# The down projection of a decoder layer as seven block products instead of eight, in three passes over the weights

## The chip, the cores and the metric

The kernel runs on one core of a Trainium2 chip. The metric is the device time in microseconds (us) of that core; a time given for a kernel is the median of several runs. Beside it stands one profiled execution of the same kernel, whose durations the prediction uses. The engines are named as the profile names them: PE is TensorE (PEld its weight loads), DVE is VectorE, ACT is ScalarE, POOL is GpSimd, and SP is the engine that issues the transfers from memory.

## What is computed

One decoder layer over 512 tokens of width 1024, in float32. Attention (two groups of heads) and its output projection come first; the change does not touch them. Then comes the MLP with a norm on both sides:

```python
D_MODEL = 1024
SEQ = 512
D_FF = 4 * D_MODEL
...
        h = h + rms_norm(mix @ w_out[l], attn_post_g[l])
        u = rms_norm(h, mlp_pre_g[l])
        a = jnp.square(jax.nn.relu(u @ w_up[l]))
        h = h + rms_norm(a @ w_down[l], mlp_post_g[l])
```

The up projection is 512x1024 by 1024x4096, the down projection 512x4096 by 4096x1024. In what follows `a` (the activations) is the left factor of the down projection and `w_down` the right one.

## The kernel before

**Three matmuls for one.** Every float32 operand is kept as a high part, rounded to the matmul's number format (fp32r), and a low part, the rest. `mm3` (L911) issues high x high, high x low and low x high into one PSUM bank. So each block of weights passes ACT, which writes the high part (`hi_part`, L388, recorded at L389), and then DVE, which subtracts it from the whole to give the low part (`lo_part`, L634, recorded at L635; `lo_scaled`, L637, recorded at L638, does it with a gain per row). The same is done to the activations.

**Up projection** (`up_step`, L590 on ACT and L878 on DVE; `up_block`, L1157 on PE). 32 blocks of 128 columns of `w_up`; each block is 24 matmuls (8 row blocks x 3) of 512 tokens. Two blocks share a chunk of weights of 1 MB. PE writes banks 0 to 3 in turn; ACT takes relu out of the bank (L599), DVE squares it into `act_sb` (L884). The factor 1/rms of the norm ahead of the MLP is not applied here. It is left out until the end of the down projection, where its square (`stat[:, 4, t, 3:4]`) multiplies the rows.

**Down projection** (`down_chunk`, L1191, and `down_rows`, L1185, on PE; `down_hi`, L608, on ACT; `down_lo`, L897, on DVE). 16 chunks of 1 MB, each 256 rows of `w_down` by all 1024 columns. A chunk gives 48 matmuls of 128x512: 4 tiles of 128 tokens x 2 row blocks x 2 column halves x 3. The results grow in all eight banks. For every chunk ACT writes `w_hi` (128x2048 elements) and `a_hi` (128x1024), DVE writes `w_lo` and `a_lo`. Both `w_hi`/`w_lo` and `a_hi`/`a_lo` have two buffers: ACT begins on chunk c when PE has ended chunk c-2 (`w_used`), that is, when PE begins chunk c-1. SP issues the transfer of chunk c+2 as soon as DVE has done the low part of chunk c. POOL has nothing to do in this stage but the small operations of the last norm.

**The end.** Per tile of 128 tokens: ACT sums the squares of both halves from the banks (`y_squares`, L576), POOL makes 1/rms (`rms`, L316), DVE multiplies and adds the residual (`scaled`, L849), SP stores.

Of the kernel before, what the change touches and what calls it, by code (L numbers as in the profile page):

```python
# [32 lines left out]
def build(nc, x, attn_pre_g, w_in, mla_q_norm_g, w_mla_q_up, mla_kv_norm_g, w_mla_kv_up, w_out,  # L33
# [21 lines left out]
    w_down_v = w_down[0].rearrange("(k p) n -> p k n", p=P)  # L55

# [16 lines left out]
    with ExitStack() as ctx:  # L73
# [17 lines left out]
        uT_hi = sb("uT_hi", [P, ND, S], F32R)  # L91
        uT_lo = sb("uT_lo", [P, ND, S], F32R)
# [130 lines left out]
        OUT_PIECES = {i: [i - 4] if i < HEADS else [2 * i - 12, 2 * i - 11] for i in range(4, 14)}  # L223

# [4 lines left out]
        def _(sp):  # L229
# [48 lines left out]
            with sp.Fori(1, NF // 4) as i:  # L278
# [19 lines left out]
        def _(pool):  # L298
# [17 lines left out]
            def rms(norm, t, n, n_sq, parts=1, by=None, squared=False):  # L316
# [58 lines left out]
        def _(act):  # L375
# [184 lines left out]
            def mlp_hi(j, r, gains=True):  # L560

                act.wait_ge(raw_in[j], (r - j) * 8 + 16)
                if gains:
                    for k in range(ND):
                        w = slice(256 * k, 256 * k + 256)
                        last = hi_part(w_hi[1 - j][:, w], raw[j][:, w], g_up[:, k:k + 1])
                else:
                    last = hi_part(w_hi[1 - j][:, :], raw[j][:, :])
# [689 lines left out]
```

## Time and profile before

| | us |
|---|---|
| median of 3 runs (610.76 to 610.95) | 610.81 |
| profiled execution, device time | 610.47 |
| profiled execution, span of the records | 608.5 |
| PE busy in it | 594.7 (98%) |
| DVE, ACT, POOL busy | 296.7, 268.0, 100.3 |
| down projection, first matmul to last | 428.1 to 602.7 |

The span is what the records of the profile cover; 2.3 us lie between it and the median and are taken to stay. An engine's busy time is an average over stages with different limits, so the stage that is changed has to be read by itself. A matmul of 512 columns is recorded with 389 ns, but successive ones start every 0.227 us, since they overlap in the array: the pace, not the recorded length, is what a matmul costs.

### The profile page before, as it was taken

What the parts mean: (1) busy time and instruction counts of PE and PEld (TensorE: products, weight loads), DVE (VectorE), ACT (ScalarE), POOL (GpSimd) and SP (SyncE); (2) the same over time, 40 slices, a digit from 0 to 9 for tenths busy, and PEclk for the clock granted to TensorE, in tenths of its full rate; (3) what the DMA queues carried; (4) which work ended last, traced back from release to release, by engine and by line L of the source; (5) the groups of instructions that cost most, each with busy time, mean ns of one, the idle gap of its engine ahead of it and who ended that gap; (6) DMA issues with size and microseconds to landing.
All of it is one profiled execution on the core that took longest, in us unless ns stands there. A gap on an engine that the chain in (4) does not pass through costs nothing.

```text
span 608.5 us, 8201 instructions
## 1 busy us (share of the span) xinstructions
PE 594.7 (98%) x2992; PEld 500.5 (82%) x2992; DVE 296.7 (49%) x587; ACT 268.0 (44%) x564; POOL 100.3 (16%) x167
## 2 busy tenths in 40 slices
PE   7999999999999999999999999999999999999996
PEld 7988898887777788998888888888888888888884
DVE  3458582788788408535433534334242332423345
ACT  5563262788898424264425344252321313213132
POOL 1153200346798101120000000000000000000011
PEclk9999999999999999999999999999999999999999
DMA  8441412000220084004232242323223131232303
GB/s 305 128 129 57 169 70 69 1 1 1 71 71 1 6 306 139 0 1 139 69 113 94 73 134 69 111 96 122 86 76 131 69 130 77 77 130 69 104 16 122
DMA packets 32826, 55.24 MB, mean 91 GB/s; under 512 B 3232, under 2 KB 21408, under 8 KB 32800
## 3 DMA queue, kind: packets, MB, share of 16 engines
q1 hardware_dynamic: 31760, 54.90, 26.9%
q8 instruction: 15, 0.25, 0.2%
q10 hardware_dynamic: 1040, 0.00, 0.1%
q14 instruction: 11, 0.09, 0.1%
HBM read 52.80 MB, written 2.10 MB: 90 GB/s over the span
## 4 chain that ended last, share of the span: by engine, by line
PE 92%; DVE 3%; ACT 2%; issue 1%; DMA 1%; SPq 0%; DVEq 0%; POOLq 0%; POOL 0%; ACTq 0%
PE bank L913 30%; PE bank L914 29%; PE bank L915 29%; PE bank L1083 2%; DVE pT_lo L635 1%; ACT probs L501 1%; DVE bank L767 1%; DMA x_sb<-in_x 1%; PE bank L919 1%; PE bank L1020 1%; PE bank L952 1%; DVE kT_lo L635 0%; PE bank L1036 0%; ACT uT_hi L389 0%; ACT pT_hi L389 0%
## 5 line engine op out<-in xcount | busy, mean ns | idle before, releaser
L913 PE MATMUL bank<-uT_hi,w_hi 128*128 128x512 f32 (+1 forms) x280 | 104.0, 371 | 0.0
L914 PE MATMUL bank<-uT_lo,w_hi 128*128 128x512 f32 (+1 forms) x280 | 103.8, 371 | 0.0
L915 PE MATMUL bank<-uT_hi,w_lo 128*128 128x512 f32 (+1 forms) x280 | 103.8, 371 | 0.0
L913 PE MATMUL bank<-w_hi,a_hi 128*128 128x512 f32 x256 | 99.7, 389 | 0.1
L914 PE MATMUL bank<-w_lo,a_hi 128*128 128x512 f32 x256 | 99.6, 389 | 0.0
L915 PE MATMUL bank<-w_hi,a_lo 128*128 128x512 f32 x256 | 99.6, 389 | 0.0
L635 DVE TENSOR_TENSOR w_lo<-w_raw,w_hi 128x2048 fp32r<-128x2048 f32 (+1 forms) x17 | 38.4, 2261 | 111.8 <-ACT w_hi L389 111.8
L389 ACT ACTIVATE w_hi<-w_raw 128x2048 fp32r<-128x2048 f32 (+2 forms) x25 | 37.0, 1490 | 118.7 <-PE bank L915 117.9
L638 DVE SCALAR_TENSOR_TENSOR w_lo<-w_raw,g_up,w_hi 128x256 fp32r<-128x256 f32 x128 | 52.1, 480 | 48.3 <-ACT w_hi L389 48.3
L599 ACT ACTIVATE relu<-bank 128x512 f32<-128x512 f32 x32 | 19.1, 598 | 98.2 <-PE bank L915 98.2
L322 POOL TENSOR_SCALAR stat<-stat 128x1 f32<-128x1 f32 x8 | 1.9, 239 | 363.9 <-ACT junk_post L414 363.9
L913 PE MATMUL bank<-w_hi,uT_hi 128*128 128x512 f32 (+1 forms) x160 | 61.9, 387 | 0.0
L915 PE MATMUL bank<-w_hi,uT_lo 128*128 128x512 f32 (+1 forms) x160 | 61.1, 382 | 0.0
L914 PE MATMUL bank<-w_lo,uT_hi 128*128 128x512 f32 (+1 forms) x160 | 61.0, 382 | 0.0
L913 PEld LDWEIGHTS bank<-uT_hi,w_hi 128*128 128x128 f32 x280 | 52.8, 188 | 9.1
L915 PEld LDWEIGHTS bank<-uT_hi,w_lo 128*128 128x128 f32 x280 | 52.8, 188 | 9.1
L914 PEld LDWEIGHTS bank<-uT_lo,w_hi 128*128 128x128 f32 x280 | 52.8, 188 | 8.9
L389 ACT ACTIVATE w_hi<-w_raw,g_up 128x256 fp32r<-128x256 f32 x128 | 52.7, 498 | 12.5 <-DMA w_raw<-in_w_up 12.2
L913 PEld LDWEIGHTS bank<-w_hi,a_hi 128*128 128x128 f32 x256 | 48.1, 188 | 10.4 <-issue 0.5
L915 PEld LDWEIGHTS bank<-w_hi,a_lo 128*128 128x128 f32 x256 | 48.1, 188 | 10.0
L914 PEld LDWEIGHTS bank<-w_lo,a_hi 128*128 128x128 f32 x256 | 48.1, 188 | 9.9
L884 DVE TENSOR_TENSOR act_sb<-relu 128x512 f32 (+1 forms) x32 | 22.1, 690 | 64.6 <-ACT relu L599 64.6
(127 smaller groups left out, 944.6 us busy)
## 6 DMA issues: line engine op xcount, KB each, us to landing
w_raw<-in_w_up SPq DMA_DIRECT2D x16, 1024.0 KB, 5.2
w_raw<-in_w_down SPq DMA_DIRECT2D x16, 1024.0 KB, 4.8
w_raw<-in_w_in SPq DMA_DIRECT2D x6, 1024.0 KB, 5.8
w_raw<-in_w_out SPq DMA_DIRECT2D x4, 1024.0 KB, 4.8
x_sb<-in_x SPq DMA_DIRECT2D x8, 256.0 KB, 5.9
h_sb<-in_x SPq DMA_DIRECT2D x4, 512.0 KB, 4.9
out<-h_sb SPq DMA_DIRECT2D x8, 256.0 KB, 2.0
w_raw<-in_w_in SPq DMA_DIRECT2D x2, 416.0 KB, 5.0
```

What stands on the lines that cost most here:

```text
L389: return nc.scalar.activation(out, whole, ACT.Copy, scale=scale)
L501: nc.scalar.activation(probs[i % 2][:, p_off(t):p_off(t) + n], ps[b][:, c:c + n], ACT.Exp, bias=nb[:, i % 2, t:t + 1], scale=-1.0, accum_o ...
L599: nc.scalar.activation(relu[:, m, :], ps[2 * j + m][:, :], ACT.Relu).then_inc(relu_c, 1)
L635: return nc.vector.tensor_tensor(out, whole, hi.bitcast(F32), ALU.subtract)
L638: return nc.vector.scalar_tensor_tensor(out=out, in0=whole, scalar=scale, in1=hi.bitcast(F32), op0=ALU.mult, op1=ALU.subtract)
L767: nc.vector.tensor_tensor_reduce(out=s, in0=s, in1=mask[:, TOP - P * (t + 1):], scale=-SCALE[i], scalar=-NEG, op0=ALU.add, op1=ALU.min, ac ...
L884: nc.vector.tensor_tensor(act_sb[:, bass.ds(i * 4 + (2 * j + m), 1), :], relu[:, m:m + 1, :], relu[:, m:m + 1, :], ALU.mult).then_inc(a_re ...
L913: nc.tensor.matmul(out, lh, rh, start=start, stop=False)
L914: nc.tensor.matmul(out, lh, rl, start=False, stop=False)
L915: return nc.tensor.matmul(out, ll, rh, start=False, stop=stop)
L919: last = nc.tensor.transpose(ps[2 * t + k // 4][:, P * (k % 4):P * (k % 4) + P], src[:, t, P * k:P * k + P], ident[:, :])
L1083: last = nc.tensor.transpose(ps[b][:, c + P * (t - k):c + P * (t - k) + P], probs[i % 2][:, p_off(t) + P * k:p_off(t) + P * k + P], ident[ ...
```

## The change

**Seven products.** The 512 tokens are split into two halves (h), the 4096 inner rows into the even and the odd blocks of 128 (m), the 1024 columns into two halves. With A[h][m] and B[m][n] the eight block products become seven, each of 256 tokens x 2048 x 512, i.e. 16 row blocks x 2 tiles x 3 = 96 matmuls of 128x512. They need sums of blocks: S3 = A11-A21, S2 = A22-S3, S1 = A11+S2, S4 = A12-S2 of the activations, and T1 = B12-B11, T3 = B22-B12, T2 = B22-T1, B21-T2 of the weights. The products are added up into the four blocks of the result at the end.

**Three passes, 28 chunks of 1 MB.** Pass 1 (chunks 0 to 7): A11 B11 and A12 B21. Pass 2 (chunks 8 to 23): four products with the sums S1, S3, S2 and A22, for which all of `w_down` is read again. Pass 3 (chunks 24 to 27): S4 B22. Each chunk is 24 matmuls. There are four buffers `w_raw` instead of two (the two more lie where the inputs `uT` of the up projection were), three of `a_hi`/`a_lo` instead of two, still two of `w_hi`/`w_lo`.

**Who makes the sums.** The weight sums of pass 2 are written in place into `w_raw`, four operations of 128x512 for a chunk: DVE makes them for chunks 8, 10, ... 22, POOL for 9, 11, ... 23. POOL makes the sums of the activations: 16 operations of 128x256 during the up projection (S3), and three of 128x512 elements for each of 8 groups after it (`token_sums`). DVE adds up the results (`combine`).

**The norm's factor.** It now has to be in the activations. Four transposes on PE spread 1/rms over a row (`r_row`), DVE takes relu times `r_row` from the bank, ACT squares. The squares of `h_sb` and POOL's work on them are moved between the tiles of the output projection. At the end the tiles are taken in the order 2, 3, 0, 1.

The diff, cut to its core:

```diff
+            def difference(c):
+                pool.wait_ge(a_ready, 2 * c + 1)
+                nc.gpsimd.tensor_tensor(pairs_of(act_sb)[:, c, 0, 1, :], pairs_of(act_sb)[:, c, 0, 0, :],
+                                        pairs_of(act_sb)[:, c, 0, 1, :], ALU.subtract).then_inc(s3_ready, 1)
+            def block_sums(c, n):
+                b11, b12, b21, b22 = (d_raw(c)[:, TOP * q:TOP * q + TOP] for q in range(4))
+                pool.wait_ge(*down_arrived(c))
+                for m, (out_b, a, b) in enumerate(((b11, b12, b11), (b12, b22, b12), (b22, b22, b11), (b21, b21, b22))):
+                    if m:
+                        pool.wait_ge(odd_sums, 4 * n + m)
+                    nc.gpsimd.tensor_tensor(out_b, a, b, ALU.subtract).then_inc(odd_sums, 1)
+            def token_sums(n):
+                a5, two = pairs_of(act_sb), slice(2 * n, 2 * n + 2)
+                pool.wait_ge(s3_ready, 2 * n + 2)
+                pool.wait_ge(up_full, NF)
+                pool.wait_ge(a_ready, 4 * n + 4)
+                nc.gpsimd.tensor_tensor(s2[:, two, :], a5[:, two, 1, 1, :], a5[:, two, 0, 1, :],
+                                        ALU.subtract).then_inc(s2_ready, 1)
+                pool.wait_ge(s2_ready, n + 1)
+                pool.wait_ge(al, n + 1)
+                nc.gpsimd.tensor_tensor(a5[:, two, 0, 0, :], a5[:, two, 0, 0, :], s2[:, two, :], ALU.add).then_inc(s_ready, 1)
+                nc.gpsimd.tensor_tensor(a5[:, two, 1, 0, :], a5[:, two, 1, 0, :], s2[:, two, :],
+                                        ALU.subtract).then_inc(s_ready, 1)
+            for c in range(N1 + 1, N1 + N2, 2):
+                while n_tok < min(N2 // 2, 5 + (c - N1 - 1) // 2 * 2):
+                    token_sums(n_tok)
+                    n_tok += 1
+                block_sums(c, (c - N1) // 2)
...
+            def down_w_hi(c):
+                act.wait_ge(*down_arrived(c))
+                if c >= N1 and c < N1 + N2:
+                    act.wait_ge((even_sums, odd_sums)[(c - N1) % 2], 4 * ((c - N1) // 2 + 1))
+                if c == 1:
+                    act.wait_ge(up_full, NF)
+                elif c >= 2:
+                    act.wait_ge(d_used, c - 1)
+                for w in (slice(0, CW // 2), slice(CW // 2, CW)):
+                    hi_part(w_hi[1 - c % 2][:, w], d_raw(c)[:, w]).then_inc(dwh, 1)
...
+                        nc.vector.scalar_tensor_tensor(out=relu[:, m, :], in0=ps[2 * j + m][:, :], scalar=0.0,
+                                                       in1=r_row[:, :], op0=ALU.max, op1=ALU.mult).then_inc(relu_c, 1)
...
+                down_w_lo(c)
+                if 3 <= c + 1 < NDOWN:
+                    down_a_lo(c + 1)
+                if N1 <= c + 2 < N1 + N2 and (c + 2 - N1) % 2 == 0:
+                    block_sums(c + 2)
...
-            down_chunk(0, 0, True)
-            down_chunk(1, 1)
-            with pe.Fori(1, NF // 4 - 1) as i:
-                down_chunk(0, i * 2)
-                down_chunk(1, i * 2 + 1)
...
+            for c in range(N1):
+                down_ready(c)
+                for q in range(4):
+                    for t in range(2):
+                        last = product((P1, P2)[q % 2], t, c, q, c == 0 and q < 2, c == N1 - 1 and q >= 2)
+                last.then_inc(d_used, 1)
+            pe.wait_ge(relu_c, NF)
+            for c in range(N1, N1 + N2):
+                down_ready(c)
```

What the change puts on DVE in the down projection shows best in the order of its instructions. Before, the loop over two chunks (two pieces of `w_lo`, two of `a_lo`):

```order
L902 UNCONDITIONAL_BRANCH
L902 ISA
L635 TENSOR_TENSOR w_lo1<-w_raw0,w_hi1 128x2048
L888 REGISTER_ALU
L635 ISA
L635 TENSOR_TENSOR a_lo0<-act_sb,a_hi0 128x1024
L835 REGISTER_ALU
L635 TENSOR_TENSOR w_lo0<-w_raw1,w_hi0 128x2048
```

Now two chunks of pass 2, of which the second is an even one ahead in the pipeline (`s2` holds S2, `w_raw0` the chunk two later):

```order
L785 TENSOR_TENSOR w_lo0<-w_raw1,w_hi0 128x1024 x2
L785 TENSOR_TENSOR a_lo0<-act_sb,a_hi0 128x512
L785 TENSOR_TENSOR a_lo0<-act_sb,a_hi0 128x256
L785 TENSOR_TENSOR a_lo0<-s2,a_hi0 128x256
L785 TENSOR_TENSOR w_lo1<-w_raw2,w_hi1 128x1024 x2
L785 TENSOR_TENSOR a_lo1<-act_sb,a_hi1 128x512
L785 TENSOR_TENSOR a_lo1<-act_sb,a_hi1 128x256
L785 TENSOR_TENSOR a_lo1<-s2,a_hi1 128x256
L1063 TENSOR_TENSOR w_raw0<-w_raw0 128x512 x4
```

The work of the loop is the same per chunk, but a chunk now feeds 24 matmuls instead of 48, and the four sums stand behind every second one.

POOL had only the small operations of the norms from here on. Now its queue reads, at the change from pass 1 to pass 2:

```order
L477 TENSOR_TENSOR act_sb<-act_sb,s2 128x2x256
L478 TENSOR_TENSOR act_sb<-act_sb,s2 128x2x256
L463 TENSOR_TENSOR w_raw1<-w_raw1 128x512 x4
L473 TENSOR_TENSOR s2<-act_sb 128x512
L477 TENSOR_TENSOR act_sb<-act_sb,s2 128x2x256
L478 TENSOR_TENSOR act_sb<-act_sb,s2 128x2x256
```

In all, 24 such operations on activations and 32 on weights stand behind the last block of the up projection, each on 512 elements per partition, each reading two tensors in SBUF.

## Rows read from the trace of the kernel before

**Rows 1.** The page: the span, and the busy time of each engine.

```profile
span 608.5 us, 8201 instructions
...
PE 594.7 (98%) x2992; PEld 500.5 (82%) x2992; DVE 296.7 (49%) x587; ACT 268.0 (44%) x564; POOL 100.3 (16%) x167
```

**Rows 2.** The page: the chain that ended last, by engine, then by line.

```profile
PE 92%; DVE 3%; ACT 2%; issue 1%; DMA 1%; SPq 0%; DVEq 0%; POOLq 0%; POOL 0%; ACTq 0%
PE bank L913 30%; PE bank L914 29%; PE bank L915 29%; PE bank L1083 2%; DVE pT_lo L635 1%; ACT probs L501 1%; DVE bank L767 1%; DMA x_sb<-in_x 1%; PE bank L919 1%; PE bank L1020 1%; PE bank L952 1%; DVE kT_lo L635 0%; PE bank L1036 0%; ACT uT_hi L389 0%; ACT pT_hi L389 0%
```

**Rows 3.** Busy time and instructions by window: the down projection.

```profile
core 0: us, PE busy (x) PEld busy (x) DVE busy (x) ACT busy (x) POOL busy (x), PEclk, DMA share, GB/s
428.10:602.70 174.60, 174.48 (x769) 143.93 (x767) 61.42 (x44) 48.98 (x45) 3.42 (x10) 1.00 0.25 90
```

**Rows 4.** Timeline, ACT then DVE, one chunk of the down projection (start, length).

```profile
482.81 1.92 ACT L389 ACTIVATE w_hi<-w_raw 128x2048 fp32r<-128x2048 f32 x1 [8.11 <-PE bank L915]
484.63 1.04 ACT L389 ACTIVATE a_hi<-act_sb 128x1024 fp32r x1
...
484.75 2.29 DVE L635 TENSOR_TENSOR w_lo<-w_raw,w_hi 128x2048 fp32r<-128x2048 f32 x1 [7.55 <-ACT w_hi L389]
486.96 1.22 DVE L635 TENSOR_TENSOR a_lo<-act_sb,a_hi 128x1024 fp32r<-128x1024 f32 x1
```

**Rows 5.** Groups of instructions by form, DVE, two inputs in SBUF.

```profile
L635 DVE TENSOR_TENSOR a_lo<-act_sb,a_hi 128x1024 fp32r<-128x1024 f32 x16 | 19.5, 1219 | 0.3 <-ACT a_hi L389 0.3
L884 DVE TENSOR_TENSOR act_sb<-relu 128x512 f32 x24 | 16.6, 690 | 46.3 <-ACT relu L599 46.3
L753 DVE TENSOR_TENSOR q_nat<-rt 128x256 f32<-128x256 f32 x4 | 1.7, 425 | 0.1
```

**Rows 6.** Groups of instructions by form, POOL.

```profile
L362 POOL TENSOR_TENSOR probs<-probs,rs 128x512 f32<-128x512 f32 x16 | 16.6, 1038 | 56.8 <-DVE rs L777 56.8
L351 POOL TENSOR_TENSOR w_lo<-w_raw,w_hi 128x512 fp32r<-128x512 f32 x8 | 10.2, 1287 | 1.3 <-ACT w_hi L389 1.3
L362 POOL TENSOR_TENSOR probs<-probs,rs 128x128 f32<-128x128 f32 x16 | 6.4, 398 | 0.0
```

**Rows 7.** Timeline from 32.6 us: DVE, four pieces, and POOL's one-element operations beside them.

```profile
32.69 2.74 DVE L638 SCALAR_TENSOR_TENSOR w_lo<-w_raw,g_in,w_hi 128x512 fp32r<-128x512 f32 x4 [4.55 <-ACT w_hi L389]
...
33.58 0.94 POOL L326 TENSOR_TENSOR stat<-stat 128x1 f32<-128x1 f32 x1
...
34.90 0.58 POOL L325 TENSOR_SCALAR stat<-stat 128x1 f32<-128x1 f32 x1
35.57 0.55 POOL L326 TENSOR_TENSOR stat<-stat 128x1 f32<-128x1 f32 x1
```

**Rows 8.** Timeline, POOL with DVE idle or reading PSUM: the same two operations.

```profile
37.64 0.19 POOL L325 TENSOR_SCALAR stat<-stat 128x1 f32<-128x1 f32 x1
37.92 0.55 POOL L326 TENSOR_TENSOR stat<-stat 128x1 f32<-128x1 f32 x1
```

**Rows 9.** Timeline from 74 us: DVE starts behind a long POOL operation.

```profile
76.09 1.29 POOL L342 TENSOR_TENSOR mk_nat<-rt 128x512 f32<-128x512 f32 x1 [1.43 <-DVE rt L713]
...
77.14 2.79 DVE L638 SCALAR_TENSOR_TENSOR w_lo<-w_raw,g_in,w_hi 128x512 fp32r<-128x512 f32 x4 [1.12 <-ACT w_hi L389]
```

**Rows 10.** The page: transfers of `w_down` (KB each, us from issue to landing).

```profile
w_raw<-in_w_down SPq DMA_DIRECT2D x16, 1024.0 KB, 4.8
```

**Rows 11.** Timeline, ACT, ahead of the up projection's first results.

```profile
258.58 1.09 ACT L389 ACTIVATE uT_hi<-bank 128x512 fp32r<-128x512 f32 x2 [5.40 <-PE bank L919]
259.55 1.06 ACT L414 ACTIVATE junk_post<-h_sb 128x1024 bf16<-128x1024 f32 x1
...
264.76 0.60 ACT L599 ACTIVATE relu<-bank 128x512 f32<-128x512 f32 x1 [0.52 <-PE bank L915]
```

**Rows 12.** The chain in order of time: eight transposes, and the last steps.

```profile
258.10 0.87 PE bank L919 x8
...
602.51 0.24 PE bank L915
602.77 0.69 ACT junk_post L414
603.73 0.26 POOL stat L325
604.03 0.60 POOLq L73
604.66 0.75 DVE h_sb L868
605.41 0.66 DVEq L73
```

More of the change, by code:

```diff
@@ L90, in build @@
         fill_to_1k = sb("fill_to_2k", [P, (5120 - 4480) // 4])
-        uT_hi = sb("uT_hi", [P, ND, S], F32R)
-        uT_lo = sb("uT_lo", [P, ND, S], F32R)
+        with ExitStack() as inputs:
+            uT_hi = sb("uT_hi", [P, ND, S], F32R, stack=inputs)
+            uT_lo = sb("uT_lo", [P, ND, S], F32R, stack=inputs)
+        raw_more = [sb(f"w_raw{i + 2}", [P, CW]) for i in range(2)]
+        s2 = sb("s2", [P, NF // 2, 2 * P])
         raw = [sb(f"w_raw{i}", [P, CW]) for i in range(2)]
@@ new lines, in block_sums @@
+            def block_sums(c, n):
[5 more added lines that the diff above has]
+                    nc.gpsimd.tensor_tensor(out_b, a, b, ALU.subtract).then_inc(odd_sums, 1)
+            for c in range(NF // 2):
+                difference(c)
@@ L557, in _, with mlp_hi @@
                     exps(i + 1, S_ORDER[n:])
-            def mlp_hi(j, r, gains=True):
+            def mlp_hi(j, r):
                 act.wait_ge(raw_in[j], (r - j) * 8 + 16)
[L563 to L568, printed above, removed]
+                for k in range(ND):
+                    w = slice(256 * k, 256 * k + 256)
+                    last = hi_part(w_hi[1 - j][:, w], raw[j][:, w], g_up[:, k:k + 1])
                 last.then_inc(wh_ready, 1)
@@ L625, in _ @@
+            act.wait_ge(comb, 2)
+            for t in LAST_ORDER:
+                for b in range(2):
+                    act.wait_ge(*y_ready(t, b))
+                    square(y_half(t, b), 5, t, b)
         @block.vector
@@ L1183, in _ @@
                         up_block(2 * j + m, j, m, slice(0, S)).then_inc(up_full, 1)
-            def down_rows(t, b, j, kk, start, stop):
-                tok = slice(P * t, P * t + P)
-                w = slice(D * kk + TOP * b, D * kk + TOP * b + TOP)
-                return mm3(ps[2 * t + b][:, :], a_hi[j][:, kk, tok], a_lo[j][:, kk, tok], w_hi[1 - j][:, w], w_lo[1 - j][:, w],
-                           start, stop)
-            def down_chunk(j, c, first=False):
-                pe.wait_ge(w_ready, c + (DOWN_CH + 1 - NO))
-                pe.wait_ge(al, c + 1)
-                for t in ((2, 3, 0, 1) if first else range(NT)):
-                    if first and t < 2:
-                        pe.wait_ge(relu_c, NF - 2 * (1 - t))
-                    for kk in range(2):
-                        for b in range(2):
-                            last = down_rows(t, b, j, kk, first and kk == 0, False)
-                last.then_inc(w_used, 1)
@@ L1218, in _, with product @@
-            pe.wait_ge(w_ready, DOWN_CH - NO + NF // 2)
-            pe.wait_ge(al, NF // 2)
-            for t in range(NT):
-                for b in range(2):
-                    if t >= 2:
-                        last_rows(t, 0, b)
-                    last_rows(t, 1, b).then_inc(y_full, 1)
+            def product(bank, t, c, q, start, stop):
+                tok, w = slice(P * t, P * t + P), slice(TOP * q, TOP * q + TOP)
+                return mm3(ps[bank[t]][:, :], a_hi[c % 3][:, q, tok], a_lo[c % 3][:, q, tok],
+                           w_hi[1 - c % 2][:, w], w_lo[1 - c % 2][:, w], start, stop)
@@ new lines, in third @@
+            def third(c, t):
+                for q in range(4):
+                    last = product(P3, t, c, q, c == N1 + N2 and q == 0, c == NDOWN - 1 and q == 3)
+                return last
+            for c in range(N1 + N2, NDOWN - 2):
+                down_ready(c)
+                for t in range(2):
+                    if c == N1 + N2:
+                        pe.wait_ge(comb, 1 + t)
+                    last = third(c, t)
+                last.then_inc(d_used, 1)
+            for c in range(NDOWN - 2, NDOWN):
+                down_ready(c)
+                last = third(c, 0)
```

305 lines of the change are left out of this document (224 added, 81 removed).

## The prediction

> **What bounds the kernel now.** First the busy times of the page [rows 1]: PE is busy 98% of a span of 608.5 us, every other engine under half. Then the chain that ended last [rows 2]: 92% of it is PE. Then the stage that is changed, by itself [rows 3]: in the 174.6 us of the down projection PE is busy 174.5 us at a granted clock of 1.00 (2.4 GHz), while DVE is busy 61.4 us, ACT 49.0 us and POOL 3.4 us. The stage holds 16 x 48 = 768 matmuls of 512 columns, so one costs 174.6 / 768 = 0.2273 us, and nothing else shows. In the timeline of one chunk [rows 4] the reader sees the cover: ACT begins a chunk of weights, DVE ends it 5.4 us later (488.18 - 482.81), and both wait about 7.5 us for PE. That slack belongs to chunks of 10.9 us; the change halves them.
>
> **What is removed.** 96 of 768 matmuls: 672 x 0.2273 = 152.7 us instead of 174.6. If PE stays the bound this is worth -21.9 us. A chunk is now 24 matmuls, 5.46 us, and there are 28.
>
> **What is added to the stage, engine by engine.** ACT per chunk: 1.92 us for w_hi (two halves now) and about 1.04 us for a_hi [rows 4], some 3.3 us with three pieces: under 5.46. Transfers: 28 MB instead of 16; the stage's share of the transfer engines was 0.25 [rows 3], so 0.25 x 174.6 / 16 = 2.7 us a megabyte, half of 5.46; one lands in 4.8 us [rows 10] with four buffers. Neither binds.
>
> DVE: lengths are 1.22 us for 1024 elements, 0.69 for 512, 0.425 for 256 [rows 5]. Back to back they follow 0.08 us sooner (w_lo is 2.29 long, a_lo starts after 2.21 [rows 4]), so 1.14, 0.61 and 0.34. From the moment PE ends the up projection to the low part of chunk 23, DVE has: 46 halves of w_lo, 52.4; a_lo of five chunks of pass 1, 5.7; a_lo of 16 chunks of pass 2 in three pieces, 16 x 1.29 = 20.6; 32 weight sums that wait for each other, 0.69 + 0.03 each, 23.0; two additions from PSUM and the last relu, 2.1. Sum 103.9 us, and PE needs 23 x 5.46 = 125.6 us for the chunks ahead of chunk 23. Per pair of chunks in pass 2 that is 4.56 + 2.58 + 2.88 = 10.0 of 10.9 us. So DVE alone would just hold.
>
> POOL: 56 operations of 512 elements with two inputs in SBUF, like L351 and L342 at 1.29 us [rows 6, 9]: 72 us, also within 125.6. Whether the change wins therefore hangs on one question: can POOL and DVE do this at the same time? All of DVE's work in this stage but 2.1 us reads two tensors in SBUF, and so does all of POOL's.
>
> **What the trace says of that.** An operation of POOL on one element takes 0.19 us (L325) or 0.55 us (L326) [rows 8]. Beside four pieces of DVE with two inputs in SBUF the same operations take 0.58 and 0.94 us [rows 7], 0.39 us more each. The L325 at 34.90 ends at 35.48; DVE's four pieces end at 35.43, the last piece being some 0.7 us long. A single element does not need 0.39 us of a shared path: it waited for DVE's current instruction to end. Beside DVE instructions that read PSUM I find no such stretch (the eight `w_lo` of L351 in the attention keep 1.29 us [rows 6]). In the other direction the trace has one case only [rows 9]: DVE starts 77.14 while POOL's operation still has 0.24 us to run, and its four pieces take 2.79 instead of 2.74 us. So POOL's operation kept DVE out no later than 0.24 - 0.05 = 0.19 us ahead of its recorded end.
>
> **The price of a POOL operation to the pair.** Not less than nothing: nothing here makes DVE faster. Upper bound 1.29 us, its whole length. My value is 1.29 - 0.19 = 1.10 us, from the nearest row [rows 9]. A lower value in the same world is the part that grows with the elements, for one large input (1038 - 398) / 384 = 1.67 ns, 0.85 us for 512 [rows 6]. The trace has no two long ones side by side, so zero stays possible and is the rival.
>
> The Trainium skill (SBUF — State Buffer, section "Who interferes with whom") says that a VectorE instruction with two SBUF inputs and a GpSimd instruction that reads SBUF contend, and that the second to issue waits until the first is done. The rows agree for POOL behind DVE (0.39 us); for DVE behind POOL only 0.05 us is to be seen. By that rule the price would be the whole 1.29 us and the time 642 us, instead of the 631 us by my 1.10.
>
> **The sum.** With turns taken, the low part of chunk 23 is ready at 1.2 (ACT's first half) + 103.9 + 56 x 1.10 = 166.7 us after the up projection. Can the two really be busy without a pause? ACT and PE do not stop them: DVE's two chunks take 10.0 + 4 x 1.10 = 14.4 us, PE's 10.9, so PE waits and frees its buffers early, and POOL always has an arrived chunk or activations to work on save some 5 us in pass 1, when it waits for chunk 9; DVE's work goes on then. PE then does chunks 23 to 27, 5 x 5.46 = 27.3 us; in pass 3 DVE needs 3.5 us a chunk and the eight additions fall beside chunks 23 and 24. The stage ends at 194.0 us instead of 174.6: +19.4 us.
>
> **The small parts.** Four transposes: 0.87 / 8 = 0.11 us each [rows 12], +0.4 us. They wait for 1/rms of the last tile: ACT ends uT_hi at 259.67, one square of h_sb takes 1.06 + 0.2, POOL 0.85, so about 262; PE ends the first block near 264.7 (ACT takes it at 264.76 [rows 11]): 2.7 us of cover. In the up projection relu now is DVE's (0.75 us) and the square ACT's; PE waits for a bank four blocks back, some 16 us, and ACT's later start on the next weights (0.8 us) stands against several us of slack: 0. POOL's 16 differences, about 0.75 us each, are kept apart from DVE's 3.3 + 1.5 us of 10.9: 0. The end: one addition (0.69) is put before the last square, and square and product lose a scale (0.09 and 0.06) on a chain of 0.69 and 0.75 steps [rows 12]: +0.6 us. Order of tiles: 0.
>
> Total +19.4 + 0.4 + 0.6 = **+20.4 us**: span 608.5 to 628.9, and with the 2.3 us between span and median 631.2. Forecast **631 us**, slower.
>
> **Rivals.**
> First, on the other side: **POOL and DVE overlap after all**. For it: [rows 9] shows DVE slowed by 0.05 us only, and POOL's one-element operations may have waited for a start and not for the data. Against it: [rows 7]. The point from which it decides: the stage is as long as before if chunk 23 starts 146.3 us in, i.e. when a POOL operation costs DVE (146.3 - 105.1) / 56 = 0.74 us; below 0.37 us PE is the bound all through. Then 610.8 - 21.9 + 1.0 = 590 us. Between 0.37 and 0.74 it gives 590 to 610.
>
> Second: **the lock is as long as the operation**, 1.29 us: + 56 x 0.19 = 10.6, 642 us. With 0.85 us it is 617.
>
> Third: **PE's clock falls**. PE now idles: in a pair of 14.4 us it works 10.9. In all of the stage before it never idled and kept 1.00 [rows 3]. If every other chunk ran at 1.2 GHz, the pair would take 5.46 + 10.9 = 16.4 us instead of 14.4; 8 pairs, +16 us, 647. Nothing in the rows shows PE after an idle stretch in this size. The Trainium skill (TensorE: Matmul & The Clock Gate, "HAM oscillation — how this bites in real kernels") describes such a fall after waits between bursts; no row here bears it out.
>
> **How the numbers follow.** Turns taken at 0.74 us or more: 0.68, and the same with the clock's fall 0.07; overlap or nearly so 0.25. Faster by over 0.2% (about what a measurement of this kernel can tell from no change) 0.22, within 0.2% 0.03, slower 0.75. The range goes from 600, which is a price of 0.54 us, to 652, the fallen clock with some of the longer lock; the full overlap at 590, 0.18, and the rest are left out.
>
> **What would show it.** Right: in the windows of pass 2 PE busy near 75% and waiting for DVE's w_lo, the pair of chunks near 14 to 15 us, DVE's and POOL's lengths stretched beside each other (POOL's 128x512 well over 1.29 us, or DVE's 128x1024 well over 1.22), pass 3 at 5.46 us a chunk. Wrong: POOL's sums at 1.29 us with DVE's at 1.22 beside them, and PE without idle time. If PE is short of w_lo with both at their old lengths, a semaphore or a transfer is late that I have counted as covered.

## The result, and the profile after

| | before | after |
|---|---|---|
| median, us (4 runs each) | 610.84 (610.76 to 610.95) | 635.17 (634.82 to 635.29) |
| span of the records | 608.5 | 633.0 |
| PE busy | 594.7 (98%) | 584.9 (92%) |
| DVE, ACT, POOL busy | 296.7, 268.0, 100.3 | 424.6, 309.9, 213.8 |
| down projection, first matmul to the end of the last | 174.6 | 194.5 (428.6 to 623.1) |

The ratio is 1.0397, with a 95% interval of 1.0379 to 1.0415: 24.3 us slower, although PE has 96 matmuls of 512 columns less to do. The forecast was 631 us.

First the page of after: the span, the busy time of each engine, PE and its clock in 40 slices, and the chain that ended last by engine. They answer to [rows 1, 2].

```profile
span 633.0 us, 8193 instructions
...
PE 584.9 (92%) x2900; PEld 486.7 (77%) x2900; DVE 424.6 (67%) x717; ACT 309.9 (49%) x651; POOL 213.8 (34%) x235
...
PE   8999999899999999999999999999877688779993
...
PEclk9999999999999999999999999999997799998998
...
PE 66%; DVE 27%; ACT 3%; issue 2%; DMA 1%; POOL 0%; SPq 0%; DVEq 0%; POOLq 0%; ACTq 0%
```

The chain had 3% of DVE; now it has 27%. POOL has 0% of it, and yet POOL is the cause, as will be seen: a chain shows who was late, not who held it up.

The same stage by windows, where [rows 3] had one line with PE busy 174.48 of 174.60. Columns: window, its length, then busy time (and instructions) of PE, PEld, DVE, ACT, POOL, the granted clock, the share of the transfer engines, GB/s.

```profile
472.00:482.00 10.00, 5.78 (x15) 4.58 (x16) 10.00 (x6) 2.96 (x5) 9.84 (x7) 0.66 0.30 105
...
516.00:530.00 14.00, 11.31 (x51) 9.04 (x50) 13.90 (x15) 6.28 (x10) 6.48 (x4) 1.00 0.46 151
...
585.40:600.00 14.60, 14.60 (x65) 11.83 (x64) 10.49 (x13) 6.76 (x7) 0.00 (x0) 1.00 0.56 185
```

At 472 to 482, the change from pass 1 to pass 2, PE is busy 5.78 of 10 us, at a mean granted clock of 0.66. 516 to 530 is as long as a pair of chunks of pass 2: DVE has no pause (13.90 of 14.00), PE is busy 81% (near 75% was forecast). From 585.4, with POOL silent, PE is full again.

What the two engines do in such a pair, from the timelines of DVE and then of POOL (start, length; a row with x4 stands for four instructions in a row), as [rows 4] had it for before:

```profile
503.79 5.79 DVE L1063 TENSOR_TENSOR w_raw<-w_raw 128x512 f32<-128x512 f32 x4
509.50 3.44 DVE L785 TENSOR_TENSOR w_lo<-w_raw,w_hi 128x1024 fp32r<-128x1024 f32 x2
...
514.15 2.35 DVE L785 TENSOR_TENSOR w_lo<-w_raw,w_hi 128x1024 fp32r<-128x1024 f32 x2
...
517.69 5.79 DVE L1063 TENSOR_TENSOR w_raw<-w_raw 128x512 f32<-128x512 f32 x4
...
503.87 6.86 POOL L463 TENSOR_TENSOR w_raw<-w_raw 128x512 f32<-128x512 f32 x4 [9.69 <-DMA w_raw<-in_w_down]
...
517.90 6.72 POOL L463 TENSOR_TENSOR w_raw<-w_raw 128x512 f32<-128x512 f32 x4 [7.16 <-DMA w_raw<-in_w_down]
```

The same two halves of `w_lo` take 2.35 us at 514.15, when POOL waits for a transfer, and 3.44 at 509.50, when it works. The pair lasts 517.69 - 503.79 = 13.9 us, and four POOL operations in it stretch DVE by 5.79 - 2.86 (the four sums alone, from the first experiment) and by 3.44 - 2.35: 4.0 us, 1.0 each.

The groups of DVE and POOL by form in the stage answer to [rows 5] (1219 and 690 ns) and [rows 6] (1287):

```profile
L1063 DVE TENSOR_TENSOR w_raw<-w_raw 128x512 f32<-128x512 f32 x32 | 46.6, 1456 | 0.8
L785 DVE TENSOR_TENSOR w_lo<-w_raw,w_hi 128x1024 fp32r<-128x1024 f32 x45 | 73.0, 1661 | 4.6 <-ACT w_hi L506 4.5
...
L463 POOL TENSOR_TENSOR w_raw<-w_raw 128x512 f32<-128x512 f32 x32 | 53.4, 1668 | 51.0 <-DMA w_raw<-in_w_down 49.2
L478 POOL TENSOR_TENSOR act_sb<-act_sb,s 128x512 f32<-128x512 f32 x8 | 16.8, 2100 | 0.0
```

DVE's 32 sums are 0.77 us longer than 0.69, the 45 halves of `w_lo` 0.44 longer than 1.22, and so on. Over the whole span DVE is busy 424.6 us; with the same list and POOL silent (experiment 1) it is busy 369.8. That makes 54.8 us for 56 operations of POOL, 0.98 each.

And what PE waited for (us in total, times, longest):

```profile
PE bank L1119 <- DVE w_lo L785: 23.5, 12, 5.7
PE bank L1119 <- DVE relu L1083: 6.5, 1, 6.5
```

The 6.5 us are not a wait for a low part. PE stands in chunk 8 for two additions (L1083) that empty a bank, and these start only at 495.37, behind the four weight sums that DVE has taken up at 489.65.

### The profile page after: what moved, and what is told of

Its sections match the earlier page's. It is cut to its first block, busy times and chain, and to the rows that moved or that the text cites. A ratio compares the mean times of both kernels' runs of the same rounds, so it can differ in the third digit from the quotient of the medians.

```text
span 633.0 us, 8193 instructions
## 1 busy us (share of the span) xinstructions
PE 584.9 (92%) x2900; PEld 486.7 (77%) x2900; DVE 424.6 (67%) x717; ACT 309.9 (49%) x651; POOL 213.8 (34%) x235
## 4 chain that ended last, share of the span: by engine, by line
PE 66%; DVE 27%; ACT 3%; issue 2%; DMA 1%; POOL 0%; SPq 0%; DVEq 0%; POOLq 0%; ACTq 0%
PE bank L1119 21%; PE bank L1121 20%; PE bank L1120 20%; DVE w_lo L785 11%; DVE w_raw L1063 7%; DVE a_lo L785 5%; PE bank L1289 2%; DVE pT_lo L785 1%; ACT probs L618 1%; DVE bank L917 1%; DMA x_sb<-in_x 1%; ACT junk_post L531 1%; DVE h_sb L1010 1%; PE bank L1125 1%; DVE s L1075 1%
## 5 line engine op out<-in xcount | busy, mean ns | idle before, releaser
L1119 PE MATMUL bank<-w_hi,a_hi 128*128 128x512 f32 x224 | 91.8, 410 | 31.0 <-DVE w_lo L785 23.5
L506 ACT ACTIVATE w_hi<-w_raw 128x1024 fp32r<-128x1024 f32 (+2 forms) x65 | 62.6, 1007 | 103.9 <-PE bank L1121 100.4
L785 DVE TENSOR_TENSOR w_lo<-w_raw,w_hi 128x1024 fp32r<-128x1024 f32 (+1 forms) x57 | 87.7, 1577 | 16.3 <-ACT w_hi L506 16.3
L1120 PE MATMUL bank<-w_lo,a_hi 128*128 128x512 f32 x224 | 89.8, 401 | 0.0
L1121 PE MATMUL bank<-w_hi,a_lo 128*128 128x512 f32 x224 | 89.6, 400 | 0.0
L1119 PEld LDWEIGHTS bank<-w_hi,a_hi 128*128 128x128 f32 x224 | 43.6, 194 | 46.8 <-DVE w_lo L785 29.3
L463 POOL TENSOR_TENSOR w_raw<-w_raw 128x512 f32<-128x512 f32 x32 | 53.4, 1668 | 51.0 <-DMA w_raw<-in_w_down 49.2
L747 ACT ACTIVATE act_sb<-relu 128x512 f32 (+1 forms) x32 | 20.2, 632 | 89.7 <-DVE relu L1053 89.7
L441 POOL TENSOR_TENSOR probs<-probs,rs 128x512 f32<-128x512 f32 (+1 forms) x64 | 44.1, 719 | 57.0 <-DVE rs L927 57.0
L454 POOL TENSOR_TENSOR act_sb<-act_sb 128x256 f32<-128x256 f32 x16 | 11.8, 739 | 152.1 <-ACT act_sb L747 152.1
```

The costliest lines, as they stand in the source:

```text
L441: nc.gpsimd.tensor_tensor(pr, pr, rs[:, i % 2, t:t + 1].to_broadcast([P, P * (t + 1)]), ALU.mult).then_inc(s_norm, 1)
L454: nc.gpsimd.tensor_tensor(pairs_of(act_sb)[:, c, 0, 1, :], pairs_of(act_sb)[:, c, 0, 0, :], pairs_of(act_sb)[:, c, 0, 1, :], ALU.subtract) ...
L463: nc.gpsimd.tensor_tensor(out_b, a, b, ALU.subtract).then_inc(odd_sums, 1)
L506: return nc.scalar.activation(out, whole, ACT.Copy, scale=scale)
L747: nc.scalar.activation(act_sb[:, bass.ds(i * 4 + (2 * j + m), 1), :], relu[:, m:m + 1, :], ACT.Square).then_inc(a_ready, 1)
L785: return nc.vector.tensor_tensor(out, whole, hi.bitcast(F32), ALU.subtract)
```

## The experiments

Each stands beside runs of the kernel before on the same chip (medians 610.65 to 610.84 us). "After" is the changed kernel. The diffs are cut to their core: semaphore counts that follow from moved work are left out. Experiments 1, 4 and 5 are single runs, so their times have no interval.

**1. POOL silent.** After without POOL's 56 operations behind the up projection.

```diff
-            n_tok = 0
-            for c in range(N1 + 1, N1 + N2, 2):
-                while n_tok < min(N2 // 2, 5 + (c - N1 - 1) // 2 * 2):
-                    token_sums(n_tok)
-                    n_tok += 1
-                block_sums(c, (c - N1) // 2)
```

> The changed kernel without GpSimd's work behind the up projection: the four sums of the odd chunks and the sums S1, S2, S4 of the activations are left out (the odd chunks go in as they are, A22 stands in for S2, S3 is still made during the up projection), so this part of the result is not the reference's. Every matmul, transfer, ScalarE and VectorE operation stays. Theory A (turns: a GpSimd operation keeps VectorE out for about 1 us): VectorE needs 103.9 us where TensorE needs 125.6, TensorE becomes the bound again, about 594 us, with VectorE's 128x1024 back at 1.22 us. Theory B (VectorE's own 104 us and its semaphore waits are too long a chain for chunks of 5.46 us, GpSimd takes no part): 610 us or more. Theory C (TensorE waits for transfers of 28 MB): 620 us or more.

Measured: 595.97 us, 39.2 less than after. The groups of this kernel by form, DVE:

```profile
L1057 DVE TENSOR_TENSOR w_raw<-w_raw 128x512 f32<-128x512 f32 x32 | 22.1, 690 | 0.8
L779 DVE TENSOR_TENSOR w_lo<-w_raw,w_hi 128x1024 fp32r<-128x1024 f32 x54 | 63.6, 1219 | 24.5 <-ACT w_hi L500 24.5
```

Both are back at the lengths of [rows 5], and PE waits for `w_lo` 1.8 us instead of 23.5. The operations of DVE and ACT, the transfers and the three passes are as in after (only ACT no longer waits for POOL's results), so none of them is the bound by itself. What this leaves open is whether POOL's *work* or the *waiting for its results* was the trouble; the next ones tell.

**2. All weight sums on DVE.** POOL keeps the sums of the activations.

```diff
-                if N1 <= c + 2 < N1 + N2 and (c + 2 - N1) % 2 == 0:
+                if N1 <= c + 2 < N1 + N2:
                     block_sums(c + 2)
```

> All weight sums on VectorE (16 chunks instead of 8), GpSimd keeps only the 24 operations of the sums of the activations. Theory A: VectorE gets 32 x 0.72 = 23.0 us more and is rid of 32 x 1.10 = 35.2 us of GpSimd, -12.2 us against the changed kernel, 623 us. Theory B (no contention, VectorE alone too slow): +23 us, 658 us. Theory C (transfers): unchanged, 635 us.

Measured: 622.73 us (622.44 to 623.15), ratio 1.0197 (1.0180 to 1.0214).

**3. All sums on DVE, POOL idle.** As 2, and `token_sums` is called on DVE, behind the low part of chunks 1 to 8:

```diff
-            for n_tok in range(N2 // 2):
-                token_sums(n_tok)
...
+                if c - 1 < N2 // 2:
+                    token_sums(c - 1)
```

> All sums on VectorE but S3 in the up projection: GpSimd does nothing between the up projection and the last norm. Theory A: VectorE gets 56 x 0.72 = 40.3 us more and is rid of 56 x 1.10 = 61.6 us of turns, -21.3 us, 614 us; pairs of chunks in pass 2 at 12.9 us. Theory B: +40 us, 675 us. Theory C: unchanged, 635 us.

Measured: 614.89 us (614.64 to 614.90), ratio 1.0068 (1.0051 to 1.0085). DVE has 56 more operations than in after, and the kernel is 20.3 us faster.

**4. All weight sums on POOL.**

```diff
-            for c in range(N1 + 1, N1 + N2, 2):
-                while n_tok < min(N2 // 2, 5 + (c - N1 - 1) // 2 * 2):
+            for c in range(N1, N1 + N2):
+                while n_tok < min(N2 // 2, 4 + c - N1):
...
-                if N1 <= c + 2 < N1 + N2 and (c + 2 - N1) % 2 == 0:
-                    block_sums(c + 2)
```

> All weight sums on GpSimd, none on VectorE: 88 GpSimd operations of 512 elements. Theory A: VectorE is rid of 23.0 us and gets 32 x 1.10 = 35.2 us of turns, +12.2 us, 647 us. Theory B (no contention): GpSimd's own 88 x 1.37 = 121 us just fit in 125.6, VectorE needs 81: TensorE is the bound, 594 us. Theory C: unchanged, 635 us.

Measured: 650.69 us. DVE, with 32 operations less than in after, shows these groups by form, and POOL this one:

```profile
L785 DVE TENSOR_TENSOR w_lo<-w_raw,w_hi 128x1024 fp32r<-128x1024 f32 x43 | 85.8, 2034 | 10.2 <-ACT w_hi L506 10.2
L785 DVE TENSOR_TENSOR a_lo<-act_sb,a_hi 128x512 fp32r<-128x512 f32 x15 | 25.5, 1700 | 0.0
...
L463 POOL TENSOR_TENSOR w_raw<-w_raw 128x512 f32<-128x512 f32 x64 | 110.1, 1727 | 8.3 <-DMA w_raw<-in_w_down 4.6
```

DVE's operation of 512 elements, 0.69 us alone, takes 1.70. Experiments 2 to 4 with after make a ladder that gives the price from the times. If an operation costs DVE 0.72 us where it makes it and a price p where POOL makes it, moving it changes the time by p - 0.72:

| moved from DVE to POOL | time | per operation | p |
|---|---|---|---|
| 3 to 2: 24 sums of activations | 614.89 to 622.73 | +0.33 | 1.05 |
| 2 to after: 32 weight sums | 622.73 to 635.17 | +0.39 | 1.11 |
| after to 4: 32 weight sums more | 635.17 to 650.69 | +0.48 | 1.20 |

On each rung giving DVE's work to a second engine made the kernel slower. The last rung holds more than turns, though. POOL's list has grown to 88 operations, ACT waits 26.4 us for its sums, and DVE stands for `w_hi` 10.2 us up to 600 us and 1.8 once more ahead of chunk 23, where it stood 4.6 in after (the `w_lo` groups above). Without these 7.5 us the last price would be about 0.97 and not 1.20, so the rise down the table does not show turns that grow dearer.

**5. The price by itself.** The kernel before, with POOL busy in the down projection on a tile that nobody else uses; each operation waits for the last.

```diff
+            pool.wait_ge(up_full, NF)
+            for n in range(24):
+                one(nc.gpsimd.tensor_tensor(dummy[:, 2, :], dummy[:, 0, :], dummy[:, 1, :], ALU.subtract))
+            for n in range(12):
+                one(nc.gpsimd.tensor_tensor(dummy[:, 2:4, :], dummy[:, 0:2, :], dummy[:, 0:2, :], ALU.subtract))
+            for n in range(24):
+                one(nc.gpsimd.tensor_scalar(dummy[:, 2, :], dummy[:, 0, :], 2.0, 1.0, ALU.mult, ALU.add))
+            for n in range(32):
+                one(nc.gpsimd.memset(dummy[:, 3, :], 0.0))
```

> The kernel before, complete, with operations on GpSimd added that touch only a tile of their own, one after another from the end of the up projection: 24 of 128x512 with two SBUF inputs, 12 of 128x1024 with two, 24 of 128x512 with one, 32 memsets of 128x512 (no input). TensorE stays the bound, 611 us. Theory A (the two take turns by whole operations, and it is reads that exclude each other): VectorE's w_lo (2.29 us) grows by up to 1.1 us beside the first kind, by up to 2.2 beside the second, by less beside the third, and not beside memsets; GpSimd's operations that meet it grow by up to 2.2 us. Theory B (they share the path element by element): every operation grows by its own part, GpSimd's and VectorE's by similar ratios whatever the length of the other. Theory C (any GpSimd operation, writes too): memsets grow as well.

Measured: 610.67 us, the time of before: PE stays the bound there, so DVE has room and the records show the price undisturbed. POOL's four streams, then DVE's low parts, two chunks in the first stream and the activations' part (1.22 us alone) in each of the others:

```profile
428.74 44.37 POOL L383 TENSOR_TENSOR dpool<-dpool 128x512 f32<-128x512 f32 x24 [161.25 <-PE bank L935]
473.20 31.96 POOL L385 TENSOR_TENSOR dpool<-dpool 128x1024 f32<-128x1024 f32 x12
505.25 22.32 POOL L387 TENSOR_SCALAR dpool<-dpool 128x512 f32<-128x512 f32 x24
527.62 18.61 POOL L389 MEMSET dpool<- 128x512 f32 x32
...
441.56 3.33 DVE L655 TENSOR_TENSOR w_lo<-w_raw,w_hi 128x2048 fp32r<-128x2048 f32 x1 [4.07 <-ACT w_hi L409]
444.81 2.31 DVE L655 TENSOR_TENSOR a_lo<-act_sb,a_hi 128x1024 fp32r<-128x1024 f32 x1
452.34 2.29 DVE L655 TENSOR_TENSOR w_lo<-w_raw,w_hi 128x2048 fp32r<-128x2048 f32 x1 [5.23 <-ACT w_hi L409]
...
477.16 2.91 DVE L655 TENSOR_TENSOR a_lo<-act_sb,a_hi 128x1024 fp32r<-128x1024 f32 x1
...
509.33 1.63 DVE L655 TENSOR_TENSOR a_lo<-act_sb,a_hi 128x1024 fp32r<-128x1024 f32 x1
...
530.81 1.22 DVE L655 TENSOR_TENSOR a_lo<-act_sb,a_hi 128x1024 fp32r<-128x1024 f32 x1
```

Beside POOL operations with two inputs of 512 elements `a_lo` takes 2.31 us, +1.09 (2.30 to 2.32 in all four chunks of this stream); with two of 1024, +1.69; with one of 512, +0.41; beside a memset, which reads nothing, nothing. `a_lo` stands right behind `w_lo`, and for the end of `w_lo` a POOL operation has been waiting: the one that starts at 442.82 is 3.21 us long instead of 1.29 and ends at 446.03, and `a_lo`, which ends at 447.12, can have begun its own 1.22 us only at about 445.9. `w_lo` itself (2.29 alone, 2048 elements) comes at any moment of a POOL operation and waits for the rest of it: its stretch is 0.36, 1.04, 0.00 and 0.03 us in the four chunks, never more than that of `a_lo` with half as many elements. So it is a turn taken per operation and not a slower rate per element: DVE waits at most once, for no more than about one POOL operation's reading, whatever its own length.

**6. Fewer and longer sums on DVE.** Since a wait between dependent operations and a start were paid per operation in 3, the first two weight sums become one of 1024 elements, and the sums of the activations are made for 4 blocks at a time (12 operations of 1024 instead of 24 of 512); the two additions that stand behind the last chunk move behind chunk 26.

```diff
+                nc.vector.tensor_tensor(b4[:, 0:2, :], b4[:, 1:4:2, :], b4[:, 0:2, :], ALU.subtract).then_inc(even_sums, 1)
+                dve.wait_ge(even_sums, 3 * n + 1)
+                nc.vector.tensor_tensor(b4[:, 3, :], b4[:, 3, :], b4[:, 0, :], ALU.subtract).then_inc(even_sums, 1)
+                dve.wait_ge(even_sums, 3 * n + 2)
+                nc.vector.tensor_tensor(b4[:, 2, :], b4[:, 2, :], b4[:, 3, :], ALU.subtract).then_inc(even_sums, 1)
```

> All sums on VectorE as in e3_dve_only, the weight sums in three operations (T1 and T3 in one of 128x1024), the sums of the activations two groups at a time (128x1024), and the two additions into the banks of P4 put behind w_lo of chunk 26 instead of behind that of chunk 27. If VectorE is the bound in pass 2 (6.3 us a chunk of 5.46): 16 x 0.23 = 3.7 us less than e3, 1 us from pass 1, 3.8 us from the end: 606 us. If it is not VectorE's time but the dependences between its operations, 614 us less only what the end gives, 611.

Measured: 608.81 us (608.66 to 609.07), ratio 0.9967 (0.9955 to 0.9980): between the two expectations, nearer the second. PE still waits for `w_lo` 6.8 us in 16 pieces, so DVE remained the bound in pass 2. Another 4.0 us PE stands at the change from pass 1 to pass 2.

**7. The end of after by itself.** The two additions moved, nothing else.

```diff
+                if c == N1 + N2 + 2:
+                    for t in range(2):
+                        dve.wait_ge(*((d_used, N1 + N2) if t else (p_full, 7)))
+                        combine(ps[P4[t]][:, :], u3(t), ps[P4[t]][:, :])
```

> The changed kernel with one thing moved: the two additions into the banks of P4 stand behind w_lo of chunk 26 instead of behind w_lo of chunk 27. If the end of the kernel is long because the norms of tiles 2 and 3 begin only with these additions: 3 to 4 us less, 631.5 us. If the end is bound by the chain behind the last matmul whatever comes before: 635 us.

Measured: 633.09 us (633.05 to 633.22), 2.1 less than after. The direction was right, the size too high.

**8. Sums between the low parts.** As 6, but each weight sum stands between two pieces of a low part, so that the wait on the previous sum is over when its turn comes, and `w_lo` is made in one piece in pass 2.

```diff
+                if more:
+                    sum_piece(c + 1, 0)
                 dve.wait_ge(ah, c + 1)
+                lo_part(lo[:, 0:2, :], a5[:, q, 0, :, :], hi[:, 0:2, :])
+                if more:
+                    sum_piece(c + 1, 1)
+                lo_part(lo[:, 2, :], a5[:, q, 1, 1, :], hi[:, 2, :])
+                last = lo_part(lo[:, 3, :], s2[:, q, :], hi[:, 3, :])
...
+                if more:
+                    sum_piece(c + 1, 2)
```

> e6_dve_merged with the order on VectorE changed in pass 2: the three weight sums of a chunk alternate with the pieces of a_lo, so that none waits for the one just before it, and w_lo is one operation of 128x2048. VectorE then needs 2.21 + 1.14 + 3 x 0.61 + 2 x 0.34 = 5.9 us a chunk instead of 6.3. VectorE's time as the bound of pass 2: 15 x 0.4 = 6 us less than e6, 600 us. Without effect if TensorE or transfers bind there: 606 us.

Measured: **604.18 us** (604.05 to 604.32), ratio 0.9891 (0.9874 to 0.9907). It beats both kernels, 6.7 us or 1.1% under before. Two things change against experiment 6, the order and the single `w_lo`; the runs do not separate them. DVE's timeline of one chunk of pass 2, and what PE waited for in the stage:

```profile
481.30 2.28 DVE L766 TENSOR_TENSOR w_lo<-w_raw,w_hi 128x2048 fp32r<-128x2048 f32 x1
483.50 1.22 DVE L1047 TENSOR_TENSOR w_raw<-w_raw 128x1024 f32<-128x1024 f32 x1
...
487.11 2.28 DVE L766 TENSOR_TENSOR w_lo<-w_raw,w_hi 128x2048 fp32r<-128x2048 f32 x1
...
PE bank L1138 <- issue: 3.7, 1, 3.7
PE bank L1138 <- DVE w_lo L766: 1.7, 3, 0.9
```

487.11 - 481.30 = 5.81 us a chunk on DVE against 5.46 on PE: nearly balanced. Of the 4.2 us above the 600, 2.8 were there already in experiment 6 (608.81 where 606 was forecast); the step from 6 to 8 gave 4.6 instead of 6. What the trace still shows: PE waits 3.7 us at the change from pass 1 to pass 2, where DVE has a group of activation sums (470.69 to 474.30) in front of `w_lo`, and the end is 1.9 us longer than before's (from the last matmul's start at 594.24 to the span's end 8.1 us, before 6.2, from 602.35).

**9 and 10. The last two tiles.** DVE makes the last addition of tile 1 only behind `h_sb` of tile 0. Here both additions come first: in 8 (experiment 9) and in 7 (experiment 10).

```diff
-                if t < 2:
-                    dve.wait_ge(y_full, 2 * NT + t + 1)
-                    combine(u2(t), u2(t), ps[P3[t]][:, :])
+                for m in range(2 if t == 0 else 0):
+                    dve.wait_ge(y_full, 2 * NT + m + 1)
+                    combine(u2(m), u2(m), ps[P3[m]][:, :])
```

> The version with all sums on DVE, one of them between two low parts, and with the last addition of tile 1 put ahead of the norm of tile 0. Theory (the end is one queue: DVE makes the last addition of tile 1 only after it has written h_sb of tile 0, which waits for POOL's 1/rms; from one such addition to the next are 4.36 us in the trace of the changed kernel, 621.81 to 626.17): with both additions first, ACT's squares and POOL's 1/rms of tile 1 run beside DVE's work on tile 0, and what tile 1 adds is DVE's own products and sums, about 2.6 us in place of 4.36. The time falls by 1.0 to 1.8 us from 604.2, to 602.4 to 603.2. Rival (the end is set by the squares on ACT or by the stores): no change, 604.2.

> The changed kernel with both edits of the end: two additions behind the low part of chunk 26 (633.1 us by itself), and the last addition of tile 1 ahead of the norm of tile 0. Theory: the same 1.0 to 1.8 us as in the other version, since the end is the same there, 631.3 to 632.1 us. Rival: 633.1, no change. If it falls, the end of the changed kernel was late by 2.1 + 1 to 2 us for the order of DVE's queue alone, out of the 4.4 us by which it is longer than before.

Measured: 604.6 us (604.49 to 605.01) instead of 604.18, and 633.68 (633.57 to 633.81) instead of 633.09: the theory failed, both are 0.4 to 0.6 us slower. The timelines of DVE, in 8 first and then in 9, show why:

```profile
594.08 1.41 DVE L991 SCALAR_TENSOR_TENSOR h_sb<-un,stat,h_sb 128x512 f32<-128x512 f32 x2 [0.80 <-POOL stat L405]
595.41 0.68 DVE L1088 TENSOR_TENSOR s<-s,bank 128x512 f32<-128x512 f32 x1
...
598.44 1.42 DVE L991 SCALAR_TENSOR_TENSOR h_sb<-un,stat,h_sb 128x512 f32<-128x512 f32 x2 [0.80 <-POOL stat L405]
```

```profile
594.58 0.69 DVE L1088 TENSOR_TENSOR s<-s,bank 128x512 f32<-128x512 f32 x1 [2.91 <-PE bank L1140]
...
596.39 1.41 DVE L991 SCALAR_TENSOR_TENSOR h_sb<-un,stat,h_sb 128x512 f32<-128x512 f32 x2
...
598.93 1.40 DVE L991 SCALAR_TENSOR_TENSOR h_sb<-un,stat,h_sb 128x512 f32<-128x512 f32 x2
```

From one `h_sb` to the next it is 2.54 us instead of 4.36, as expected (2.6). But PE ends tile 1 only at about 594.5, and DVE stands still for 2.91 us in front of that addition with tile 0's norm behind it, which in 8 was done in just that time: tile 0 is 2.3 us later (596.39 against 594.08), and the end 0.5. I had read the order of DVE's queue and not when PE delivers.

## Why the prediction was right

By its own steps, with the stage's start at 428.6 and the last matmul's end at 623.1:

| term | predicted | measured |
|---|---|---|
| ahead of the stage | +0.4 | +0.5 |
| start of chunk 23 behind the up projection | 166.7 | 164.8 |
| chunks 23 to 27 | 27.3 | 29.7 |
| stage | 194.0 (+19.4) | 194.5 (+19.9) |
| the end | +0.6 | +4.1 |
| sum | +20.4 | +24.5 |

(PE's timeline has the first matmul of chunk 23 at 593.45.)

**PE gives back 21.9 us: right, and visible only once nothing else binds.** In pass 3 a chunk takes 5.46 us when PE has no wait in it. With POOL silent the stage takes 155.5 us (428.8 to 584.3), 19.1 less than before, and the kernel comes to 596 us. Experiment 8 gets 6.7 us of it in earnest.

**DVE's own list would just hold: right.** With POOL silent (experiment 1) PE waits for `w_lo` 1.8 us in all. POOL's 56 operations on top, made by DVE (experiment 3), are too much in this form: PE waits 11.1 us for `w_lo`.

**Turns, at 1.10 us a POOL operation: right in kind, a tenth too dear.** Experiment 5 measured 1.09 where one operation of DVE's stands right behind another and POOL never pauses; the ladder's two clean rungs give 1.05 and 1.11. In after itself it is 0.98 to 1.0, and a pair took 13.9 us instead of 14.4; not every operation of POOL meets DVE in full, as `w_lo` in experiment 5 shows. The value came from a single pair of rows [rows 9] by subtraction, 1.29 - 0.19; the one-element operations of [rows 7, 8] gave the mechanism, and they were the better evidence.

**That 631 lies within 4 us of 635 is partly luck.** By the sum, DVE would end the low part of chunk 23 after 166.7 us. It ended it after 163.1 (591.75). The cheaper turns make 56 x 0.12 = 6.7 us less; against them DVE stood some 4 us for `w_hi`, which the sum had as covered, most of it in two waits, 1.88 us at 435.35 and this one in front of chunk 23 itself:

```profile
589.39 2.36 DVE L785 TENSOR_TENSOR w_lo<-w_raw,w_hi 128x1024 fp32r<-128x1024 f32 x2 [2.19 <-ACT w_hi L506]
```

PE took chunk 23 up only at 593.45, since it still had chunks 21 and 22 to do: at the end of pass 2 PE was the bound again. So the first 166.7 us came out 1.9 too long, and pass 3 and the end, below, 5.9 too short.

**The rival of overlap** (590 us) falls with experiments 1 and 5. Its 590 was also out of reach in this form: with POOL silent it is 596, since the longer end is there too. **The rival of the longer lock** (1.29 us, 642 us) falls too, by little: +1.09. The Trainium skill (SBUF — State Buffer, section "Who interferes with whom") says that DVE with two inputs in SBUF and POOL reading SBUF contend, and that one which only writes does not. By that rule, and not by a cost for any POOL work, the memsets of experiment 5 should be free: the trace agrees, 1.22 us. The wait of the full length that the prediction took from it was not seen: DVE was let in 0.1 to 0.2 us ahead of the recorded end (about 445.9 against 446.03 in experiment 5), as in [rows 9].

**The rival of the clock** (647 us): it happened, and cost next to nothing. The timeline of PE behind its waits:

```profile
476.22 0.80 PE L1119 MATMUL bank<-w_hi,a_hi 128*128 128x512 f32 x1 [5.65 <-DVE w_lo L785]
476.81 0.63 PE L1120 MATMUL bank<-w_lo,a_hi 128*128 128x512 f32 x1
...
554.66 0.50 PE L1119 MATMUL bank<-w_hi,a_hi 128*128 128x512 f32 x1 [2.71 <-DVE w_lo L785]
...
568.55 0.50 PE L1119 MATMUL bank<-w_hi,a_hi 128*128 128x512 f32 x1 [2.71 <-DVE w_lo L785]
...
570.16 0.63 PE L1119 MATMUL bank<-w_hi,a_hi 128*128 128x512 f32 x1
...
582.44 0.50 PE L1119 MATMUL bank<-w_hi,a_hi 128*128 128x512 f32 x1 [1.11 <-DVE w_lo L785]
```

A matmul at 1.2 GHz is recorded with 0.63 us and follows every 0.427 us, at 2.4 GHz with 0.39 and every 0.227. Behind the waits of 5.65 and 6.50 us PE did 11 or 12 at the lower level, and 8 behind one of the four waits of about 2.7 us, but none behind the other three. That is 31 x 0.2 = 6.2 us of PE. Yet the pair at 554.66 and the pair at 568.55 last 13.89 us both: in the second the clock took 1.6 us, and the next wait for `w_lo` was shorter by as much, 1.11 instead of 2.71. DVE set the pace and the slow matmuls fell into PE's waiting. The rival's sum had added the slow clock on top of a pair that DVE bounds; it should have been put beside it.

**Pass 3** took 2.4 us more than 27.3. The eight additions do stand beside chunks 23 and 24, as counted, but in front of `w_lo` of chunk 25 (DVE runs them from 598.22 to 603.00), and PE stood for it until 605.41. "Beside" was taken for "free" on the engine's busy time alone, without asking what they are queued in front of. The second wait, until 614.75 for `w_lo` of chunk 27, is not theirs: DVE stood 2.44 us in front of that piece for ACT's `w_hi`, whose buffer comes free only when PE ends chunk 25, and PE asks for chunk 27 after the first half of chunk 26, because the last two chunks are taken tile by tile.

**The end is the term that was mis-sized**, +0.6 against +4.1. DVE's timeline in after, where [rows 12] had one product, a square and `h_sb`:

```profile
614.62 1.28 DVE L1075 TENSOR_TENSOR bank<-s,bank 128x512 f32<-128x512 f32 x2
...
624.84 1.42 DVE L1010 SCALAR_TENSOR_TENSOR h_sb<-un,stat,h_sb 128x512 f32<-128x512 f32 x2 [0.80 <-POOL stat L405]
626.17 0.68 DVE L1075 TENSOR_TENSOR s<-s,bank 128x512 f32<-128x512 f32 x1
...
629.20 1.41 DVE L1010 SCALAR_TENSOR_TENSOR h_sb<-un,stat,h_sb 128x512 f32<-128x512 f32 x2 [0.80 <-POOL stat L405]
```

PE ends tile 1 at 623.1, and its addition starts at 626.17: 3.1 us late, behind the norms of tiles 2, 3 and 0 in DVE's queue, which could begin only behind the two additions at 614.62. From the addition to `h_sb` it is 3.03 us, where before it was 1.9 from the square to `h_sb` (602.77 to 604.66 [rows 12]), +1.1; together +4.1. The prediction counted the addition's length and not its place. Experiment 7 undoes the part that comes from the two additions (2.1 us; the addition of tile 1 then starts at 624.37); 9 and 10 say that the rest is not to be had by that swap.

## What to carry to other kernels

Before giving VectorE's elementwise work to GpSimd, look whether both read two SBUF tensors: here each GpSimd operation held VectorE up for 1.0 to 1.1 us, more than the 0.7 us that VectorE would have needed for it, so offloading made the bound engine slower. Taking all of them back won 20 us; fewer and longer operations, placed so that each dependent one has another between it and its input, won 11 more. A product saved on the engine that bounds is worth only what the feeding engine lets through: of 21.9 us saved on TensorE, experiment 8, with 5.81 us a chunk on VectorE against 5.46, kept 6.7; and in a queue the place of an operation counts, both what stands in front of it and what its wait holds up behind it.

## What the hardware showed that I had not expected

- The length of DVE's operation does not set the wait: one with 2048 elements is stretched by 1.04 us at most, one with 1024 by 1.09, and the short ones of 512 in experiment 4 by 1.0. The stretch follows POOL's operation: 0.41 us with one input of 512 elements, 1.09 with two, 1.69 with two of 1024, none for a memset.
- POOL pays as well: its operation of 1.29 us takes 1.67 in after and 1.73 in experiment 4, one group of its activation sums (L478) 2.10 on average.
- Waits of 2.7 us in front of PE had the granted clock fall once in four times, for 8 matmuls; what sets the one apart from the other three stays open.
